# Head outputs of an attention stage normed with the tokens on the partitions, and the queries' Newton step on GpSimd

## The reference

```python
def _rms(x, g):
    y = x * lax.rsqrt(jnp.mean(x * x, axis=-1, keepdims=True) + EPS)
    return y * g
q = _rms((xm @ w_q).reshape(B, T, 8, 2, 64), q_g) * 64 ** -0.5   # norm of each half head
p = softmax(q @ k^T + bias, masked)                              # two maps per head
a = p[:, :, 0] - lam * p[:, :, 1]
o = a @ v                                                        # 8 heads of 128 columns
o = _rms(o, head_g) * (1 - lam_init)                             # norm of each head's output
x = x + g1 * (o @ w_o)
```

## Time and profile before

| | us |
|---|---|
| median of 3 runs | 1470.33 (1469.79 to 1470.41) |
| the profiled execution | 1470.15 |
| its span in the trace | 1468.4 |

### The profile page before, as it was taken

One profiled execution on the slowest core, in us unless ns is written; L12 is line 12 of the kernel. 1 busy time (PEld: TensorE's weight loads), 2 busy tenths in 40 slices (PEclk: granted clock), 3 DMA queues, 4 the chain that ended last, 5 costly groups with the idle time before them and its releaser, 6 DMA issues.

```text
span 1468.4 us, 29233 instructions
## 1 busy us (share of the span) xinstructions
PE 1444.8 (98%) x11236; PEld 1368.3 (93%) x11236; DVE 1048.7 (71%) x1862; ACT 427.6 (29%) x906; POOL 759.3 (52%) x513
## 2 busy tenths in 40 slices
PE   6999999999999999999999999999999999999999
PEld 4987899999999999999999887778999999999998
DVE  5897665567776877776688347886966779476698
ACT  5303454211110011112232147774421133111132
POOL 2445343555555455555545444567565556555554
PEclk9999999999999999999999999999999999999999
DMA  9573222244456544444222252231222222222222
GB/s 377 177 254 133 89 87 74 87 157 151 166 200 214 194 144 162 153 169 138 83 92 72 84 190 89 89 103 38 79 85 73 86 94 79 89 84 86 86 90 104
DMA packets 57531, 183.50 MB, mean 125 GB/s; under 512 B 6440, under 2 KB 9904, under 8 KB 57440
## 3 DMA queue, kind: packets, MB, share of 16 engines
q1 hardware_dynamic: 54432, 179.25, 35.7%
q10 hardware_dynamic: 3008, 3.01, 0.6%
HBM read 171.69 MB, written 10.55 MB: 124 GB/s over the span
## 4 chain that ended last, share of the span: by engine, by line
PE 90%; DVE 5%; issue 1%; DMA 1%; ACT 1%; POOL 0%; SPq 0%; ACTq 0%; DVEq 0%; POOLq 0%
PE psum L779 62%; PE psum L845 7%; PE psum L1054 7%; PE psum L1253 3%; PE psum L1345 1%; PE psum L1188 1%; DMA ada_first<-in_ada_w 1%; PE psum L1308 1%; PE psum L1060 1%; DVE w_ring L2581 1%; DVE act_lo L2013 1%; PE psum L1295 1%; PE psum L1291 1%; PE psum L790 1%; PE psum L816 1%
## 5 line engine op out<-in xcount | busy, mean ns | idle before, releaser
L658 POOL TENSOR_SCALAR w_hi<-raw 128x1024 fp32r<-128x1024 f32 (+1 forms) x168 | 192.0, 1143 | 574.4 <-PE psum L779 478.3
L662 POOL TENSOR_TENSOR w_lo<-raw,w_hi 128x1024 fp32r<-128x1024 f32 (+2 forms) x195 | 440.5, 2264 | 14.0
L779 PE MATMUL psum<-act_hi,w_hi 128*128 128x288 f32 (+1 forms) x1952 | 424.8, 299 | 1.3 <-issue 0.6
L779 PE MATMUL psum<-act_hi,w_lo 128*128 128x288 f32 (+1 forms) x1952 | 420.9, 297 | 0.0
L779 PE MATMUL psum<-act_lo,w_hi 128*128 128x288 f32 (+1 forms) x1952 | 420.5, 297 | 0.0
L779 PEld LDWEIGHTS psum<-act_hi,w_hi 128*128 128x128 f32 x1952 | 315.5, 190 | 6.4 <-issue 4.0
L779 PEld LDWEIGHTS psum<-act_hi,w_lo 128*128 128x128 f32 x1952 | 316.0, 189 | 0.0
L779 PEld LDWEIGHTS psum<-act_lo,w_hi 128*128 128x128 f32 x1952 | 315.3, 189 | 0.0
L779 PE MATMUL psum<-hid_both,w_hi 128*128 128x288 f32 x704 | 122.9, 297 | 0.0
L1960 DVE SCALAR_TENSOR_TENSOR psum<-ada_quad,cst,psum 128x512 f32<-128x512 f32 x168 | 112.8, 748 | 0.0
L779 PEld LDWEIGHTS psum<-hid_both,w_hi 128*128 128x128 f32 x704 | 103.5, 189 | 1.2 <-issue 1.2
(11 more groups left out here) (383 smaller groups left out, 2457.2 us busy)
## 6 DMA issues: line engine op xcount, KB each, us to landing
raw<-in_w_stream SPq DMA_DIRECT2D x153, 512.0 KB, 3.5
ada_quad<-in_ada_w SPq DMA_DIRECT2D x56, 512.0 KB, 4.5
raw<-in_w_down SPq DMA_DIRECT2D x32, 704.0 KB, 4.1
ada_first<-in_ada_w SPq DMA_DIRECT2D x8, 1024.0 KB, 14.2
ada_ring<-in_ada_w SPq DMA_DIRECT2D x14, 512.0 KB, 4.4
ada_more<-in_ada_w SPq DMA_DIRECT2D x10, 512.0 KB, 5.3
line_rep<-line SPq DMA_DIRECT2D x8, 352.0 KB, 4.5
line<-line_rep SPq DMA_DIRECT2D x8, 352.0 KB, 5.2
```

What stands on the lines that cost most here:

```text
L658: pool.tensor_scalar(hi, src, 1.0, 0.0, ALU.mult, ALU.add).then_inc(hi_split, 1)
L662: last = pool.tensor_tensor(lo[:, c:c + w], src[:, c:c + w], hi[:, c:c + w].bitcast(F32), ALU.subtract)
L779: last = mm(psum[:, b + half, 0:n_cols], weights[wp][:, k, :], parts[ap][:, k, half * HT:half * HT + n_cols], start=(k == 0 and n == 0), s ...
```

## The change

**Head outputs.** `att_values` gives the weights as the stationary operand and the values as the moving one, so that a head's output lies with its tokens on the partitions. `att_sums` and `att_sums_sample` go. Instead ScalarE squares the head in five blocks with an accumulator (`out_squares`) and makes z and the guess on [128, 5]; VectorE makes one Newton step on [128, 5] (`out_root`, in s = 3); ScalarE scales the five blocks (`out_norm`, s = 3); TensorE turns them by four transposes at the end of s = 4 (`out_turn`) and a fifth in s = 0 of the next head (`out_turn_sample`); ScalarE copies them back (`out_back`, `out_back_sample`). Outputs alternate between PSUM banks 5 and 6, and `out_tile` takes its banks in another pairing and another order.

**GpSimd in the attention.** It no longer makes the outputs' roots. It makes the queries' Newton step (`query_root`: three pairs of half-width products and one scale-and-add) and rounds heads 0 to 5 (`round_head`).

**VectorE.** `query_newton` goes, and of `query_finish` only the last product is left; it stands in s = 4 behind `att_weight`, no longer in s = 3. `query_second(2)` moves to g = 3. The root of head 7 is the small one too.

**Elsewhere.** The first six products of unit U_O are issued ahead of the waits at the mixer's start; of the eight state stores two go out in head 4, two in head 5 and four in head 7; GpSimd splits seven of the eight tiles of unit U_OUT+2 before unit U_OUT is done (`split_behind`); units U_FFN0, U_AO+3, U_AO+4 and U_AO+5 are split in four pieces.

```diff
+o_sample = tmp[0:TS, 3, P:2 * P]
+q_root, heads_normed = hn_dve, H
+o_bank = lambda h: 5 + h % 2
+o_banks = ((5, 7), (4, 6))
...
+    def split_behind(u0, but_last_used):
+        pool.wait_ge(raw_in[u0 % 2], 16 * (u0 // 2 + 1))
+        but_last_used()
+        for k0, k1 in ((0, KT - 1), (KT - 1, KT)):
+            src = raw[:, u0 % 2, k0 * P:k1 * P]
+            hi, lo = (w_parts[u0 % 2][part][:, k0:k1].rearrange("p k c -> p (k c)") for part in range(2))
+            if k1 == KT:
+                pool.wait_ge(unit_done, u0 - 1)
+            last = pool.tensor_scalar(hi, src, 1.0, 0.0, ALU.mult, ALU.add)
+            if k1 < KT:
+                steps(last)
+                steps.wait()
+            else:
+                last.then_inc(hi_split, 1)
+                pool.wait_ge(hi_split, u0 + 1)
+            if k1 < KT:
+                pool.wait_ge(lo_ready[A_HN], H)
+            last = pool.tensor_tensor(lo, src, hi.bitcast(F32), ALU.subtract)
+        last.then_inc(lo_split, 1)
...
-    split_pairs(3, 26)
+    split_pairs(3, (U_OUT - 1) // 2)
+    split_behind(U_OUT + 2, lambda: pool.wait_ge(turned, H))
+    split_unit(U_OUT + 3)
+    split_pairs(U_OUT + 4, 2)
+    split_unit(U_FFN0, pieces=4)
+    split_unit(U_FFN0 + 1)
+    split_pairs(U_FFN0 + 2, 10)
...
+    def query_root(n):
+        pool.wait_ge(kz_ready, H + n + 1)
+        pool.wait_ge(ky_ready, H + n + 1)
+        if n > 2:
+            pool.wait_ge(k_ready, H + n)
+        def by_half(out, a, b):
+            pool.tensor_tensor(out[:, 0:HT], a[:, 0:HT], b[:, 0:HT], ALU.mult)
+            return pool.tensor_tensor(out[:, HT:T], a[:, HT:T], b[:, HT:T], ALU.mult)
+        steps(by_half(tq, yq, yq))
+        steps.wait()
+        steps(by_half(tq, tq, zq))
+        steps.wait()
+        steps(pool.tensor_scalar(tq[:, :], tq[:, :], -0.5, 1.5, ALU.mult, ALU.add))
+        steps.wait()
+        by_half(yq, tq, yq).then_inc(q_root, 1)
...
+    def round_head(h):
+        pool.wait_ge(ov_ready, 2 * h + 2)
+        if h == 1:
+            pool.wait_ge(av_done, 20)
+        elif h == 4:
+            pool.wait_ge(unit_done, U_AO)
+        pool.tensor_scalar(head_part(0, h), o_place[h][:, :], ahg, 0.0, ALU.mult, ALU.add).then_inc(hi_ready[A_O], 1)
     for h in range(-1, H):
         split_unit(U_AQ + 3 + h, pieces=4)
+        for done in {2: (0,), 4: (1, 2), 5: (3,), 6: (4,), 7: (5,)}.get(h, ()):
+            round_head(done)
+        if 1 <= h < H - 1:
+            query_root(h + 1)
         if h + 1 < H:
             pool.wait_ge(stream_in[(h + 1) % 2], 80 * ((h + 1) // 2 + 1))
             pool.memset(bias_p[(h + 1) % 2][0:64, 448:512], NEG).then_inc(mask_ready, 1)
         if h == H - 1:
-            split_unit(U_AO + 3)
...
-        if h >= 1:
-            z, y, t, o = (tmp[:, n, :] for n in (1, 2, 3, 5))
...
-            steps.wait()
-            by_half(o_place[h - 1][:, :], t, o).then_inc(ov_ready, 1)
...
-    split_pairs(121, 2)
+            split_unit(U_AO + 3, pieces=4)
+    for u0 in range(U_AO + 4, U_AO + 8):
+        split_unit(u0, pieces=4 if u0 < U_AO + 6 else 1)
...
     pe.wait_ge(vones, 1)
...
             core_turn(h - 1)
         project(U_O + h, 0, act[0], bank=0, k0=6)
...
-                last = mm(psum[:, 5, qt * P:(qt + 1) * P], v_sb[h // 4][:, kt, h % 4 * P:(h % 4 + 1) * P],
-                          atr[:, g % 2, kt * P:(kt + 1) * P], start=(kt == 0), stop=(kt == qt))
+                last = mm(psum[:, o_bank(h), qt * P:(qt + 1) * P], atr[:, g % 2, kt * P:(kt + 1) * P],
+                          v_sb[h // 4][:, kt, h % 4 * P:(h % 4 + 1) * P], start=(kt == 0), stop=(kt == qt))
...
-                last = mm(psum[:, 4, 448:512], w, atr[0:n, g % 2, kt * DK:(kt + 1) * DK], start=(kt == 0), stop=(kt == 4))
+                last = mm(psum[0:TS, 4, 384:512], atr[0:n, g % 2, kt * DK:(kt + 1) * DK], w, start=(kt == 0), stop=(kt == 4))
...
-    def att_sums(h):
...
-        mm(psum[:, 6, :], mean_sq, tmp[:, 0, 0:TP], start=True, stop=True)
...
-    def att_sums_sample(h, late=False):
...
-        mm(psum[:, 4, 448:512], mean_sq, tmp[:, 0, TP:T], start=True, stop=True).then_inc(oms_ready, 1)
+    def out_turn(h):
+        pe.wait_ge(on_ready, h + 1)
+        for j in range(4):
+            last = pe.transpose(psum[:, o_bank(h), j * P:(j + 1) * P], hn[j], ident)
+        last.then_inc(o_turned, 1)
+    def out_turn_sample(h):
+        pe.wait_ge(ov_ready, 2 * h + 1)
+        pe.transpose(psum[:, o_bank(h), 0:TS], hn[4], ident[0:TS, 0:TS]).then_inc(o_turned, 1)
...
-        elif s == 3 and p >= 1 and not late:
-            att_sums(p - 1)
-        if s == 3 and p >= 1 and not late:
-            att_sums_sample(p - 1)
+        elif s == 0 and p >= 2:
+            out_turn_sample(p - 2)
...
+        if s == 4 and 1 <= p < H:
+            out_turn(p - 1)
     for f in parts:
+        if f == 15:
+            out_turn(H - 1)
...
+    out_turn_sample(H - 1)
...
+    for k, j in ((0, 0), (1, 0), (2, 0), (0, 1), (1, 1), (2, 1), (3, 0), (3, 1)):
         if j == 0:
             pe.wait_ge(lo_ready[A_O], 5 + k)
...
+            pe.wait_ge(ov_ready, 2 * H)
+        last = out_tile(4, j, k, o_banks[j], k == 0, k == 3)
...
-        if h == H - 1:
-            sa.wait_ge(state_out, 4)
-            for a in range(2):
-                r = slice(a * DK, (a + 1) * DK)
-                for n in range(2):
-                    sa.dma_start(cp_out.rearrange("d (p a e) -> d p a e", a=2, e=129)[:, 2 * n:2 * n + 2, a, :],
...
+        for n, a in {4: ((0, 0),), 5: ((0, 1),), H - 1: ((1, 0), (1, 1))}.get(h, ()):
+            sa.wait_ge(state_out, 2 * n + 2)
+            r = slice(a * DK, (a + 1) * DK)
+            sa.dma_start(cp_out.rearrange("d (p a e) -> d p a e", a=2, e=129)[:, 2 * n:2 * n + 2, a, :],
+                         cp_sb[n][r, :, :]).then_inc(state_stored, 16)
+            sa.dma_start(cs_out.rearrange("d (p a e) -> d p a e", a=2, e=129)[:, 2 * n:2 * n + 2, a, :],
+                         cs_sb[n][r, :, :]).then_inc(state_stored, 16)
...
+            sa.wait_ge(on_ready, h)
+        af(o_sample, psum[0:TS, 4, 384:512], ACT.Copy).then_inc(o_out, 1)
...
+    def out_squares(h):
         sa.wait_ge(o_out, h + 1)
...
-        af(tmp[:, 0, :], tmp[:, 5, :], ACT.Square).then_inc(osq_ready, 1)
...
+        for j in range(TT):
+            src = psum[:, o_bank(h), j * P:(j + 1) * P] if j < 4 else o_sample
+            n = P if j < 4 else TS
+            last = af(hn[j], src, ACT.Square, accum_out=ssq[0:n, j:j + 1])
+        steps(last)
         steps.wait()
-        af(tmp[:, 2, :], tmp[:, 2, :], ACT.Exp, scale=-0.5).then_inc(oy_ready, 1)
-    def head_hi(h):
+        steps(af(z5, ssq, ACT.Identity, bias=EPSC, scale=1.0 / P))
+        steps.wait()
+        steps(af(y5, z5, ACT.Ln))
+        steps.wait()
+        af(y5, y5, ACT.Exp, scale=-0.5).then_inc(oy_ready, 1)
...
+    def out_norm(h):
+        sa.wait_ge(of_ready, h + 1)
+        for j in range(TT):
+            src = psum[:, o_bank(h), j * P:(j + 1) * P] if j < 4 else o_sample
+            n = P if j < 4 else TS
+            last = af(hn[j], src, ACT.Copy, scale=f5[0:n, j:j + 1])
+        last.then_inc(on_ready, 1)
+    def out_back(h):
+        sa.wait_ge(o_turned, 2 * h + 1)
         if h == 0:
             sa.wait_ge(kv_stored, 192)
...
+        elif h < H - 1:
+            sa.wait_ge(lo_ready[A_O], 1)
+        else:
+            sa.wait_ge(lo_ready[A_O], 4)
+        af(o_place[h][:, 0:TP], psum[:, o_bank(h), :], ACT.Copy).then_inc(ov_ready, 1)
+    def out_back_sample(h):
+        sa.wait_ge(o_turned, 2 * h + 2)
+        af(o_place[h][:, TP:T], psum[:, o_bank(h), 0:TS], ACT.Copy).then_inc(ov_ready, 1)
...
-    hi_at = {(2, 2): 0, (4, 3): 1, (4, 4): 2, (5, 2): 3, (6, 2): 4, (7, 2): 5}
...
+            out_squares(p - 1)
         elif s == 3 and out:
-            z_prompt(p - 1)
+            out_norm(p - 1)
         elif s == 4 and out:
-            head_guess(p - 1)
...
+            out_back(p - 1)
+        if s == 0 and p >= 2:
+            out_back_sample(p - 2)
...
-    def query_newton(n):
-        ve.wait_ge(kz_ready, H + n + 1)
-        ve.wait_ge(ky_ready, H + n + 1)
-        steps(tt_(tq[:, :], yq[:, :], yq[:, :], ALU.mult))
-        steps.wait()
-        steps(stt(out=tq[:, :], in0=tq[:, :], scalar=-0.5, in1=zq[:, :], op0=ALU.mult, op1=ALU.mult))
     def query_finish(n):
-        steps.wait()
-        steps(stt(out=yq[:, :], in0=tq[:, :], scalar=1.5, in1=yq[:, :], op0=ALU.add, op1=ALU.mult))
-        steps.wait()
+        ve.wait_ge(q_root, heads_normed + n - 1)
         stt(out=q_sb[:, n % 2, :], in0=kf[:, n % 2, :], scalar=qgs, in1=yq[:, :],
             op0=ALU.mult, op1=ALU.mult).then_inc(k_ready, 1)
...
+    def out_root(h):
+        ve.wait_ge(oy_ready, h + 1)
+        if h >= 1:
+            ve.wait_ge(on_ready, h)
+        newton(y5, z5, t5, f5).then_inc(of_ready, 1)
...
-    lo_at = {(2, 4): 0, (5, 0): 1, (5, 1): 2, (6, 0): 3, (7, 0): 4, (7, 4): 5}
```

(36 more changed lines are left out.)

102 lines of the change are left out of this document (23 added, 79 removed).

## The result

| | before | after |
|---|---|---|
| time, median of 6 runs each, us | 1470.41 | 1482.8 (1481.6 to 1483.4) |
| ratio, 95% interval | | 1.0081 [1.0072, 1.0091] |
| profiled execution, us | 1470.15 | 1481.63 |
| its span, us | 1468.4 | 1479.7 |
| mean granted clock of TensorE | 0.998 | 0.995 |

The kernel is 12.4 us slower. Forecast were 1473.0, with a range to 1476.5: the sign of the forecast's sum is right, its size is not.

The account below looks back on a forecast made before the run. The prediction took TensorE's own stream, busy 1444.8 of 1468.4 us, as the bound. Terms -1.7 + 6.6 + 0.3 - 1.0 - 1.4 = +2.8 on 1470.15 gave 1472.95, said as 1473.0, range 1466.5 to 1476.5.

Parts of the forecast that it names:

- head 5: Attention head 5: ScalarE's squares and scaled copies delay the turn and the fourth tile's weights, +0.3 us, 0 to +1.0.
- head 6: Attention head 6: 0.69 us of work goes and some 0.3 of waits for VectorE's wide Newton step, -1.0 us.
- head 7 and the end of the loop: Last head to loop end: two pairs of sums go, two turns come, -1.1; shorter waits, -0.3; together -1.4 us.
- The wait for `q_sb`: Ends of heads 1 to 4: TensorE waits 1.54 us for VectorE's late product; each head 0.85 us longer without collision.
- The collision: Step s = 4, heads 1 to 4: GpSimd's rounding, issued into `att_weight`'s product, holds VectorE's next product for 0.79 us.
- GpSimd comes first: Rival, chance 0.20, 1475.1 us: rounding issued before `att_weight`'s product holds both products, about 0.5 us more in four heads.
- The work taken off a head: Per attention head on TensorE: sums' products and filler, 1.30 us, go; turns of 0.61 come; net -0.69 us.
- The sample's value products: Attention heads: operands exchanged, costed at nothing, -0.3 to +0.3 us per head; costing more than now would refute the prediction.
- the sample's turn: Fifth transpose, of 64 columns, per head: taken at 0.12 us in a row of transposes, some 0.3 if alone.
- The bound for ScalarE's chain: Head 5: delay from ScalarE's squares and scaled copies, estimated at +0.3 us, bounded from 0 to +1.0.
- Elsewhere: Outside attention: six products at mixer's start -0.75, split in advance at 256 us -0.65, ScalarE's stores -0.3; together -1.7 us.
- no wait for `q_sb`: Rival, chance 0.15, 1463.1 us: TensorE never waits for `q_sb`, heads 1 to 4 give 2.8 us, sum -7.2.

Follow-up runs that it names:

- the collision taken out: Kernel after, but GpSimd begins the split of heads 2 to 7 only when VectorE has written that head's `q_sb`: 1474.9 us, ratio 1.0033.
- the late product alone: Kernel before, with only VectorE's last product, which writes `q_sb`, moved from s = 3 to s = 4 behind `query_second` and `att_weight`: 1484.4 us, ratio 1.0102.
- spare products added: The late product alone, plus 14 TensorE products that nobody reads at the starts of heads 2 to 5: 1479.9 us, ratio 1.0063.
- the three moves: Kernel after, with `q_sb` written first in s = 4, splits held until behind `att_weight`, and GpSimd's queries' root ahead of the outputs' rounding: 1468.4 us, ratio 0.9982.

## Why the prediction was wrong

The spans differ by 1479.7 - 1468.4 = +11.4 us. By stage, against the terms of the sum:

| stage | predicted | measured | the rest |
|---|---|---|---|
| up to the attention's start | -1.7 | -0.9 | +0.8 |
| heads 1 to 4 | +6.6 | +11.9 | +5.3 |
| head 5 | +0.3 | +2.4 | +2.1 |
| head 6 | -1.0 | -1.1 | -0.1 |
| head 7 and the end of the loop | -1.4 | +0.5 | +1.9 |
| the rest of the kernel | 0 | -1.4 | -1.4 |
| sum | +2.8 | +11.4 | +8.6 |

The step of the prediction that weighs most is one that it put at nothing: it priced the new waits of TensorE as waits alone, with the clock fixed. The runs showed three falls of the clock behind them, 4.4 us. Behind it come the work taken off the heads, the last heads, the parts elsewhere, and in two heads the order of two instructions.

**The wait for `q_sb`: right.** The sum said 1.54 us at the starts of heads 2 to 5 without a collision, and that nothing fills it. With the collision taken out it is 1.47 to 1.78. By the same steps the late product alone should wait 2.0; it waited 2.06 each time.

**The collision: right in two heads, the other order in two.** The forecast had GpSimd's rounding issued into `att_weight`'s product, holding the one behind for 0.79. So it is ahead of heads 2 and 5: 0.77. Ahead of heads 3 and 4 the rounding came 0.18 and 0.06 us before `att_weight`'s product, and both were held, for 1.11 and 1.22. That is the rival "GpSimd comes first", and its price, 0.5 more a head; measured are 0.32 and 0.43 more, 0.75 in all. It had said that it decides from a landing 1.4 us behind the last filler product. Measured from the start of that product, `att_weight`'s product starts at 1.54 to 1.70, and the rounding at 1.92, 1.52, 1.48 and 2.17. A margin of 0.1 us was given 0.45 against 0.20, and deserved even chances. The prediction named the Trainium skill's "SBUF — State Buffer", section "Who interferes with whom", where issue order decides who blocks the other for the whole instruction. The traces agree on the order; in size the held product grew by 0.77 in the forecast's order, by the row and not by the whole rounding, and by 0.77 ahead of head 4 too, where 0.98 of the rounding was left.

**The granted clock: missed.** No term of the sum, no rival and no bound had it. The prediction read the earlier trace rows, saw the clock in the top tenth in all 40 slices, and took it as fixed; but that row describes a stream that never pauses for more than 1.2 us in the attention, and the forecast itself put pauses of 2.3 us into it. Three falls cost 4.4 us: two in heads 3 and 4, 3.0 of the 5.3 missing there, and one in head 5. The waits hold 1.1 more (10.4 us in four, 9.3 forecast).

**The work taken off a head: mis-sized.** Without its wait and its fall, a head of 1 to 4 takes 19.41, 19.54, 19.57 and 19.71 us, where 19.18 was worked out: 1.5 us in four heads. With the two above that is 5.6; the table has 5.3 because the four heads took 19.92 on average before, and the sum started from 19.87. Two terms can be read. The sample's value products were costed at nothing, within 0.3 either way: the step s = 2, in which they stand, grew from 3.59 to 3.76 us, 0.09 of it within these products (1.29 to 1.38). That they cost more was a sign by which the prediction said it would fall. And the sample's turn was taken at 0.12, as if in a row of transposes, but it stands alone between filler and turn, and the step s = 0 in which it stands grew from 2.80 to 3.13 us. Its upper bound, 0.3, was the value.

**Head 5: two terms missed.** The bound for ScalarE's chain reached to +1.0, and the wait on L1361 for its scaled copies is 0.89. But the prediction looked in this head only at `query_second`, which does not stand in its s = 4. The late product does, behind `att_weight`, and TensorE waits 0.69 for it at the start of head 6. With one fall of the clock: 19.27 - 0.69 + 0.89 + 0.69 + 1.5 = 21.66, measured 21.70.

**Head 6: right,** -1.1 against -1.0, and for the reason given: with the Newton step back on VectorE the head takes 21.43.

**Head 7 and the end: mis-sized.** From the head's start to the FFN's start, 64.9 us after and 64.4 before, TensorE's waits are 1.99 us (0.79, 0.69 and 0.51) and were 1.50: +0.5 where -0.3 was said. The work, the rest, didn't fall at all, where -1.1 was said. The stretch has two turns and three of the sample's, each of which stands alone; the sum had two turns and none of the others.

**Elsewhere: one term of three failed, and one was lost again.** Of the 0.89 us by which the attention starts earlier, 0.31 stands in the trace at 90 us already, ahead of anything that was changed. The six products at the mixer's start gave 0.58 (0.75 said): the wait of 0.69 is gone, but the six take 0.24 longer than it, and the projection that they were taken from is 0.80 shorter. ScalarE's stores gave 0.31 (0.3 said). At 300 us 0.33 goes again: TensorE comes 1.25 earlier to a product that needs VectorE's `act_lo`, which is done only 0.08 earlier. The split in advance gave 0.07. The gap at 256 us is gone, and a wait for VectorE stands in the same place:

```profile
254.48 1.07 DVE L2067 SCALAR_TENSOR_TENSOR x<-psum,mod,x 128x288 f32 x3 [0.49 <-DVE tmp L2032]
...
255.69 0.51 PE L819 MATMUL psum<-act_hi,w_hi 128*128 128x288 f32 x2 [0.56 <-DVE x L2067]
```

The products need a bank that VectorE frees at 255.55. The prediction had removed the wait that ended last without asking which one ends next.

**The rest of the kernel.** Behind the attention after is 1.4 us shorter, in code that the change doesn't touch. It is no effect of the change but one of before's traced execution: from the second feed-forward to the end, the traces of all eleven other kernels are 0.5 to 1.4 us shorter than it, among them the kernel before with the late product alone (1.1) and with spare products added (0.9). Without it and without the 0.31 us ahead of the mixer the sum would be 13.1, not 11.4; the medians differ by 12.4.

**What stays open.** The rival "no wait for `q_sb`", 1463.1, was nearly built by the three moves: they end at 1468.4, 5 us higher. The traced execution took 1467.0, which is 3.9 higher. In it, head 7 and the end (2.1), the elsewhere (1.1), heads 1 to 4 (1.4) and head 5 (0.7) are longer than that rival had them, head 6 is 0.4 shorter, and the rest is 1.0 shorter than in before's trace. Between that execution and the median are 1.4 us that no trace covers. Why heads 1 to 4 take 78.4 us and not 77 is open beyond the two terms above.

## What to carry to other kernels

A new pause of TensorE had two prices in these traces: the pause, and what the clock lost behind it. Where a forecast puts a new pause of a microsecond or two into an otherwise dense stream of TensorE, the fall belongs into the sum or among the rivals; and where the pause can't be avoided, work that nobody needs can be cheaper than none (3.4 and 4.6 us here). Before an instruction is moved behind others on its engine, list what else stands there until the end of the step: here one product of 0.82 us, placed behind `att_weight`, cost 13.5 us more than in front of them. And for each wait that a change removes, look up which of the instruction's other waits ends next.
